# GpSimd makes four more low parts, of differential attention's tenth and last projection chunk and of its output projection's first two chunks

## The reference

```python
q, k, v = split_cols(h @ w_in, [D_MODEL, D_MODEL, D_MODEL])
q = rms_norm(q.reshape(bsz, seq, nh, 2, dh), g_q)      # nh = 8 heads, dh = 64
k = rms_norm(k.reshape(bsz, seq, nh, 2, dh), g_k)
q, k = rope(q), rope(k)
# per head: two softmaxes, a = softmax(q1 k1) - lam * softmax(q2 k2)
# o = a @ v, rms_norm(o, g_sub) * (1 - lambda_init), then @ w_out
```

## Time and profile before

| | us |
|---|---|
| median of 3 executions | 1042.6 (1042.19 to 1042.66) |
| the profiled execution | 1041.08 |
| its span, first to last instruction | 1039.3 |
| PE busy | 1032.9 (99%) |
| PE weight load busy | 910.6 (88%) |
| DVE busy | 729.4 (70%) |
| ACT busy | 596.2 (57%) |
| POOL busy | 57.4 (6%) |
| low parts on DVE (line 1860) | 371.3, 172 of them |
| low parts on POOL (line 2703) | 32.3, 7 of them |

### The profile page before, as it was taken

One profiled execution on the slowest core, in us unless ns is written; L12 is line 12 of the kernel. 1 busy time (PEld: TensorE's weight loads), 2 busy tenths in 40 slices (PEclk: granted clock), 3 DMA queues, 4 the chain that ended last, 5 costly groups with the idle time before them and its releaser, 6 DMA issues.

```text
span 1039.3 us, 15837 instructions
## 1 busy us (share of the span) xinstructions
PE 1032.9 (99%) x6396; PEld 910.6 (88%) x6396; DVE 729.4 (70%) x867; ACT 596.2 (57%) x750; POOL 57.4 (6%) x53
## 2 busy tenths in 40 slices
PE   9999999999999999999999999999999999999998
PEld 8998999888888889888888888889998888888887
DVE  6888877675565568965766666677989676666665
ACT  6677545554444467765644444576777664444464
POOL 0000001200000030002006000010000200000010
PEclk9999999999999999999999999999999999999999
DMA  9655354646546545455456555455524455465641
GB/s 311 222 179 191 123 203 137 208 162 204 200 166 212 189 143 202 129 184 179 165 198 209 184 181 203 161 195 171 163 82 162 132 203 202 164 207 186 210 166 41
DMA packets 129336, 185.33 MB, mean 178 GB/s; under 512 B 3312, under 2 KB 102896, under 8 KB 129264
## 3 DMA queue, kind: packets, MB, share of 16 engines
q1 hardware_dynamic: 128416, 183.27, 52.4%
q10 hardware_dynamic: 688, 0.53, 0.2%
q0 software_dynamic: 160, 0.52, 0.2%
HBM read 183.26 MB, written 1.05 MB: 177 GB/s over the span
## 4 chain that ended last, share of the span: by engine, by line
PE 97%; DVE 1%; DMA 0%; ACT 0%; issue 0%; SPq 0%; DVEq 0%
PE PS L422 95%; PE PS L430 2%; DMA RAW<-in_w_in_dram 0%; DVE SC L2544 0%; DVE WL L1867 0%; ACT AR L1743 0%; DVE AR L2566 0%; DVE HS L2593 0%; DVE O L2601 0%; DVE AR L2539 0%; ACT WH L1243 0%; DVE AR L2532 0%; DVE X L1969 0%; ACT AR L1679 0%; DVE AR L2469 0%
## 5 line engine op out<-in xcount | busy, mean ns | idle before, releaser
L1860 DVE TENSOR_TENSOR WL<-RAW,WH 128x2048 fp32r<-128x2048 f32 (+2 forms) x172 | 371.3, 2162 | 109.4 <-ACT WH L1243 108.7
L1243 ACT ACTIVATE WH<-RAW 128x2048 fp32r<-128x2048 f32 (+2 forms) x181 | 327.8, 1812 | 85.4 <-PE PS L422 74.4
L422 PE MATMUL PS<-WH,X 128*128 128x512 f32 (+1 forms) x1104 | 302.7, 355 | 0.0
L422 PE MATMUL PS<-O,WH 128*128 128x512 f32 (+1 forms) x880 | 239.1, 361 | 0.0
L422 PEld LDWEIGHTS PS<-WH,X 128*128 128x128 f32 x1104 | 195.8, 189 | 29.9 <-issue 1.9
L422 PE MATMUL PS<-X,WH 128*128 128x256 f32 (+1 forms) x864 | 200.0, 330 | 1.5 <-DVE X L1975 1.5
L422 PE MATMUL PS<-WL,X 128*128 128x512 f32 (+1 forms) x552 | 194.6, 353 | 0.0
L422 PEld LDWEIGHTS PS<-O,WL 128*128 128x128 f32 x744 | 134.4, 189 | 22.7
L422 PE MATMUL PS<-O,WL 128*128 128x256 f32 x744 | 153.2, 280 | 0.0
L422 PE MATMUL PS<-WH,O 128*128 128x512 f32 (+1 forms) x464 | 141.0, 378 | 0.1
L422 PEld LDWEIGHTS PS<-O,WH 128*128 128x128 f32 x880 | 137.6, 190 | 3.3 <-issue 0.3
(11 more groups left out here) (222 smaller groups left out, 778.4 us busy)
## 6 DMA issues: line engine op xcount, KB each, us to landing
RAW<-in_ffn_w_in_dram SPq DMA_DIRECT2D x44, 1024.0 KB, 5.1
RAW<-in_w_ff_dram SPq DMA_DIRECT2D x32, 1024.0 KB, 5.4
RAW<-in_ffn_w_out_dram SPq DMA_DIRECT2D x22, 1024.0 KB, 5.1
RAW<-in_w_in_dram SPq DMA_DIRECT2D x18, 1024.0 KB, 5.4
RAW<-in_gla_w_in_dram SPq DMA_DIRECT2D x12, 1024.0 KB, 5.3
RAW<-in_diff_w_in_dram SPq DMA_DIRECT2D x12, 1024.0 KB, 5.2
RAW<-in_ple_w_gate_dram SPq DMA_DIRECT2D x8, 1024.0 KB, 4.9
RAW<-in_w_out_dram SPq DMA_DIRECT2D x4, 1024.0 KB, 5.2
```

The lines of the kernel that those rows point to most:

```text
L422: return e.matmul(o, l, r, start=start, stop=stop, skip_group_check=skip)
L1243: act(high, raw, ACT.Copy).then_inc(s["w_hi"], 1)
L1860: e.tensor_tensor(low, raw, high.bitcast(F32), ALU.subtract).then_inc(s["w_lo"], 1)
```

## The change

The list `POOL_LO` grows by the chunks d0+9, d0+11, d0+12 and d0+13. Through `lo_done` the waits of PE and SP on these chunks go to w_lop, and all later counts of w_lo shrink by the number of chunks taken out. DVE's `lo` does nothing for a chunk in the list; its calls for d0+9 and d0+11 stay in the text and issue nothing. The four calls of `lo_half` and the function itself go. POOL issues the four low parts, in order of the chunks, behind that of `ple_w_gate0` and ahead of its wait for df_o.

```diff
-POOL_LO = [AT["w_o_hg"] + 1, AT["w_ff1"] + 1, AT["gla_w_in"] + 1, AT["ffn_w_in0"] + 1, AT["ple_w_gate0"] + 1, AT["ffn_w_in1"] + 1, AT["ple_w_gate1"] + 1]
+POOL_LO = [AT["w_o_hg"] + 1, AT["w_ff1"] + 1, AT["gla_w_in"] + 1, AT["ffn_w_in0"] + 1, AT["ple_w_gate0"] + 1, *(AT["diff_w_in"] + n for n in (9, 11, 12, 13)), AT["ffn_w_in1"] + 1, AT["ple_w_gate1"] + 1]
...
-    def lo_half(c, x):
-
-        raw, high, low = (y[:, 1024 * x:1024 * x + 1024] for y in m.chunk(c))
-        e.wait_ge(s[landed(c, 0)[0]], landed(c, 0)[1])
-        e.wait_ge(s["w_hi"], hi_done(c)[1])
-        i = e.tensor_tensor(low, raw, high.bitcast(F32), ALU.subtract)
-        if x:
-            i.then_inc(s["w_lo"], 1)
...
     difference(4)
-    lo_half(d0 + 12, 0)
     maxima(6)
     out_sums(0)
     coefficients(5)
-    lo_half(d0 + 12, 1)
     out_factors(0)
     out_norm(0)
     difference(5)
     maxima(7)
-    lo_half(d0 + 13, 0)
     out_lo(0)
-    lo_half(d0 + 13, 1)
     out_sums(1)
...
     lo(AT["ple_w_gate0"] + 1)
+    for n in (9, 11, 12, 13):
+        lo(AT["diff_w_in"] + n)
     e.wait_ge(s["df_o"], 8)
     p_rows(1)
```

## The result

The changed kernel takes 1059.04 us (median of 5, 1057.71 to 1059.44) against 1042.6 (median of 5 by then, 1042.19 to 1043.59): ratio 1.0157, 95% interval 1.0146 to 1.0168, slower by 16.4 us. The forecast was 1054.6 with a range of 1047 to 1059.5. Its profiled execution took 1057.71 with a span of 1055.9, 16.6 above that of before.

The account below looks back on a forecast made before the run. PE was taken to bound the differential-attention stage, so its waits are kernel time; holds of DVE by POOL's four low parts add 3.8+1.4+3.3+1.6+2.3-0.3 = 12.1 us, forecast 1042.6+12.0 = 1054.6, range 1047 to 1059.5.

Parts of the forecast that it names:

- one row of 822 ns: DVE addition of 128x2, median 152 ns, once 822, ending with POOL's multiplications: read as a hold of 0.67 us.
- the 2404 ns of the table products: Slowest of POOL's 32 products of 128x64, usually 320 ns, beside a DVE low part: POOL waited for DVE.
- Rival A: No hold worth the name at the four places: PE late nowhere, gains 0.3 to 0.9 us, 1042.0; chance 0.12.
- all four steps: POOL's low parts of d0+9, d0+11, d0+12, d0+13 each hold DVE; PE late 3.8, then 1.4, 3.3+1.6, 2.3 more.
- Walked holds: DVE's products beside d0+9 stand 4.6 us; the factors of heads 4, 5 and 7 stand 3.5, 3.9 and 3.2.
- the walk: Lateness followed through the four POOL low parts: PE late 3.8, 5.3, 8.4 to 8.6, 10.0, 12.0 us at five waits.
- The sum of the holds, 12.1: PE's added waits over the stage: 3.8+1.4+3.3+1.6+2.3-0.3 = 12.1 us.
- Rival B: The hold is real, but two of the four fall into cover and cost nothing: +4 to +8, about 1049; chance 0.12.
- The gain of 0.3 at turn_a(5): PE's earlier 0.3 us wait before turn_a(5) goes, as DVE's half low part before out_lo(0) is gone.
- rival C: Two long PE stops each bring a stretch at 1.2 GHz, costing 1.9+2.4 us, in all 1059; chance 0.08.

Follow-up runs that it names:

- extra_tt: Kernel before, plus a useless GpSimd two-input subtraction of 128x2048 from SBUF at each of the four points; 1054.17 us, ratio 1.0109.
- extra_set: Kernel before, plus GpSimd filling a 128x2048 SBUF region twice with a constant at each of the four points; 1042.04 us, ratio 0.9995.
- the four single kernels: Kernel before with the low part of d0+9, d0+11, d0+12 or d0+13 alone moved to GpSimd; 1047.67, 1045.23, 1045.92, 1044.55 us.
- swap: Kernel before with DVE's out_lo(0) put ahead of both halves of the low part of d0+13; 1043.05 us, ratio 1.0007.
- gated13: Kernel before with the low part of d0+13 alone moved to GpSimd, started only behind DVE's factor of head 7; 1042.58 us, ratio 1.0.
- pieces: Changed kernel with each of GpSimd's four new low parts cut into four instructions of 512 columns; 1053.02 us, ratio 1.0095.
- only11: Kernel before with the low part of d0+11 alone moved to GpSimd; 1045.23 us, ratio 1.0024.
- fill: Changed kernel with extra matmuls on PE ahead of the waits of turn_q(2) and turn_q(3); 1055.54 us, ratio 1.0122 against the kernel before.
- only13: Kernel before with the low part of d0+13 alone moved to GpSimd, without any gate; 1044.55 us, ratio 1.0023.
- only12: Kernel before with the low part of d0+12 alone moved to GpSimd; 1045.92 us, ratio 1.0033.

## Why the prediction was right, and the step that was too small

- *PE bounds the stage, so each microsecond of its waiting is kernel time, and nothing is given back later.* Right: the tail is 222.15 against 222.16, and behind turn_a(5) nothing more was lost: it starts 15.79 late (58.12 us behind maxima(2), 42.33 before), and the stage ends 15.76 late.
- *The two engines exclude each other for a whole POOL instruction, from one row of 822 ns and the 2404 ns of the table products.* Right: every held instruction ended with POOL's; extra_tt and extra_set show it without anything else changed. In the fourteen profiles together, 51 VectorE instructions with two SBUF inputs start inside a GpSimd subtraction or product that still has longer to run than they take by themselves, and all 51 stand until it is over. Rival A is out. The Trainium skill's rule (SBUF — State Buffer, "SBUF: two separate sides") gave 4.6 us where the held row alone gave a hold of 0.7; the trace agrees with the rule, 4.42 us over the four products and holds of 3.6, 4.2 and 3.1 us on the three factors. Its further condition, that a VectorE instruction with two SBUF inputs is excluded only by a GpSimd instruction that reads SBUF, agrees with extra_set (694 ns at most).
- *Which instructions stand and what PE waits for.* Right in all four steps: the products, then the factors of heads 4, 5 and 7, and the waits at turn_q(2), scores(5), turn_q(3), turn_k(3) and turn_a(5). Walked holds 4.6, 3.5, 3.9, 3.2; measured 4.4, 3.6, 4.2, 3.1. The lateness at all five places stands in the table above: within 0.3 us of the walk while the clock was kept at 1.00.
- *The sum of the holds, 12.1.* Right: 12.13 with the clock kept at 1.00. Rival B, two of the four in cover, is out; the four single kernels show each of them costing 1.85 us of stage or more.
- *The gain of 0.3 at turn_a(5)* was not there to be had. I put PE's short wait before it down to DVE's half low part; swap shows that out_lo(0) could not have started earlier, for ACT's high part was only just there.
- **The failed step: the clock was priced at nothing in the forecast and at a chance of 0.08 in rival C.** The forecast was 12.0 us, the measurement 16.4, and the range held it only because it took in C. The clock is a term of the sum, not an alternative to it: 10.2 us at 1.2 GHz, 3.6 us of stage. Rival C had 4.3 for it and said 1059 against the measured 1059.04, that close in part by chance, for with the measured term it is 1042.6+12+3.6 = 1058.2. The 0.8 that is left has no run that prices it; the two profiles differ by 0.85 ahead of the stage, where executions of one kernel differ as well. I had let the lack of a row (longest PE idle 1.5 us) count against it, though the walk itself made PE stand 3.8 us, longer than any wait in the trace of before. The Trainium skill (TensorE: Matmul & The Clock Gate, "What's actually happening"), whose rule halves the clock after an idle window, agrees with the 0.5 behind the 3.5 us wait of turn_q(2); the runs also have falls and stays of the clock that no single length of a wait explains, listed in the last section.

## What to carry to other kernels

Before work goes from VectorE to GpSimd, look at what VectorE does beside it: in these runs a GpSimd instruction that reads SBUF stopped every VectorE instruction with two SBUF inputs until it ended, however small, so 4.6 us of "free" GpSimd time can cost more than the 2.3 us that it saves; beside VectorE work with an input in PSUM, or behind the last waited-for instruction (gated13), it cost nothing that could be measured. One odd maximum in a line of eight equal instructions was the sign of it in the trace of before; how long a hold can get that row did not show. And when a forecast makes TensorE stand for microseconds that it never stood before, the granted clock belongs in the sum.

## What the runs showed of the hardware that I had not expected

- A GpSimd fill of SBUF, harmless to two-input instructions, did hold another kind of VectorE instruction. In extra_set one instruction of a line that takes 0.17 us in every other profile took 0.55 and ended (756.76) with the second of two GpSimd fills (753.07+3.67 = 756.74). It is a TENSOR_SCALAR with one SBUF input, and this is the only case in the traces:

```profile
753.07 3.67 POOL L2753 MEMSET SCR<- 128x2048 bf16 x2 [72.66 <-ACT WH L1244]
```

```profile
756.21 0.55 DVE L2519 TENSOR_SCALAR SC<-SC 128x8 f32<-128x8 f32 x1
```

- Between two GpSimd instructions in a row VectorE gets the ports, and between two of VectorE's GpSimd does: the engines alternate, one instruction each (pieces: POOL's pieces 1.74 us beside the products instead of 1.27, DVE's products 1.78 instead of 0.69).
- The clock also fell behind single short waits, and not always. It fell for 3.4 us behind one of 1.8 us at scores(5) in only11 and in fill, and not behind the same 1.8 us in the changed kernel; in extra_tt it kept 1.00 behind 2.5 us (turn_q(2)) and fell at the wait of 2.3 us (turn_a(5)). In only13 (1.9 us) and only12 (1.2 and 1.5) it kept 1.00 in the profiled execution. So the length of the wait does not decide it, and the two groups of only13's executions suggest that not even the kernel does. What tells these cases apart the runs don't show.
- A GpSimd subtraction of 2048 columns took 3.60 us with a bf16 result and one repeated input of 512 columns, where the low part takes 4.62 with a 4-byte result. Which of the two differences does it was not tried.
